# Two transformer blocks on one core: hi/lo pairs in SBUF start at multiples of 256 bytes instead of 128, and rows of the convolution's tile have 516 words instead of 515

## The reference

```python
def second_block(x, c, ...):
    for layer in range(2):
        x = sandwich(x, c_act, mixer, ...)   # layer 0: even_mixer, layer 1: odd_mixer
        x = sandwich(x, c_act, mlp, ...)     # square(relu(h @ w1)) @ w2, hidden width 4096
def even_mixer(h, w_in, ...):
    z, xbc, dt_raw, q, k, v = split_cols(h @ w_in, EVEN_SPLITS)
    y_ssd = ssd_mixer(z, xbc, dt_raw, ...)   # xbc = silu(causal_depthwise_conv(xbc, conv_w, conv_b)), 4 taps
    y_diff = diff_attention(q, k, v, ...)
    return concatenate([y_ssd, y_diff]) @ w_out
def odd_mixer(h, w_in, ...):
    rq, rk, rv, rg, sq, sk, sv = split_cols(h @ w_in, ODD_SPLITS)
    return concatenate([retention(rq, rk, rv) * silu(rg), sliding_window_attention(sq, sk, sv)]) @ w_out
```

## The kernel before

| pair | starts (hi, lo) | over a multiple of 512 | used by |
|---|---|---|---|
| `w_hi`, `w_lo` | 16896, 33280 | 0 | all |
| `hT`, first block | 91136, 107520 | 0 | first block |
| `oT` | 132096, 144384 | 0 | first block |
| `w_out_more` | 160640, 177024 | 384 | output projection, first block, twice |
| `xT`, `aT`, `w_more` | 170240, 190720, 194816 and on | 256 | experts |
| `hT`, second block (right) | 212864, 196480 | 384 | even projection, `conv_projection`, both `mlp`, odd projection |
| `normedT`, first (about 1974 to 2024 us) | 103552, 119936 | 128 | `norm_projection` after `diff_attention` |
| `normedT`, second (2256 to 2317 us) | 136448, 152832 | 256 | `norm_projection` after `ssd` |
| `normedT`, third (2949 to 3002 us) | 193664, 210048 | 128 | `norm_projection` after retention |
| `soT` | 136320, 144512 | 128 | `window_projection`, 96 matmuls |
| `hid` | 103424, 119808 | 0 | both `mlp` |

## Time and profile before

### The profile page before, as it was taken

How to read it: one execution, slowest core, us unless ns; L and a number is a source line. 1 busy time by engine, 2 the same in 40 slices (tenths; PEclk the granted TensorE clock), 3 DMA queues, 4 the chain that set the end, 5 groups by cost and what they waited for, 6 DMA issues and landing times. The chain is left out here.

```text
span 3482.8 us, 39412 instructions
## 1 busy us (share of the span) xinstructions
PE 3102.3 (89%) x14919; PEld 2518.6 (72%) x14919; DVE 2226.9 (64%) x3130; ACT 1231.3 (35%) x1668; POOL 391.4 (11%) x152
## 2 busy tenths in 40 slices
PE   4998989995799889999399799789999898889999
PEld 3877769774677778877386578668887687758887
DVE  6756674997676667698534646666665565554445
ACT  2234233774325224467223624431112322331112
POOL 0000001000000000000000000314443000014443
PEclk9999999997899999999599999889999899979999
DMA  7754633996645742799452042124442452113222
GB/s 255 248 193 147 221 116 120 408 403 252 233 146 186 243 164 87 305 398 364 175 184 69 25 139 91 55 91 142 139 142 84 141 174 76 55 49 97 96 91 78
DMA packets 284711, 581.81 MB, mean 167 GB/s; under 512 B 21241, under 2 KB 129473, under 8 KB 277500
## 3 DMA queue, kind: packets, MB, share of 16 engines
q1 hardware_dynamic: 272168, 535.90, 44.1%
q10 hardware_dynamic: 7764, 26.85, 1.9%
q0 software_dynamic: 4608, 16.78, 1.3%
HBM read 527.50 MB, written 78.71 MB: 174 GB/s over the span
## 5 line engine op out<-in xcount | busy, mean ns | idle before, releaser
L138 ACT CAST w_hi<-ring 128x2048 fp32r<-128x2048 f32 (+3 forms) x156 | 289.1, 1856 | 1174.2 <-PE ps L290 1037.3
L290 PE MATMUL ps<-hT_hi,w_hi 128*128 128x512 f32 (+1 forms) x1256 | 501.4, 399 | 27.3 <-DVEq L1124 16.0
L290 PE MATMUL ps<-hT_lo,w_hi 128*128 128x512 f32 (+1 forms) x1256 | 496.5, 395 | 0.0
L145 POOL TENSOR_TENSOR w_lo<-ring,w_hi 128x2048 fp32r<-128x2048 f32 x64 | 306.7, 4793 | 907.5 <-ACTq L3205 525.4
L150 DVE TENSOR_TENSOR w_lo<-ring,w_hi 128x2048 fp32r<-128x2048 f32 (+3 forms) x104 | 226.9, 2186 | 183.4 <-ACT w_hi L138 183.1
L290 PE MATMUL ps<-hT_hi,w_lo 128*128 128x512 f32 (+1 forms) x1256 | 306.3, 396 | 5.9 <-DVE w_lo L150 5.9
L290 PEld LDWEIGHTS ps<-hT_hi,w_hi 128*128 128x128 f32 (+1 forms) x1256 | 238.5, 190 | 87.4 <-DVEq L1124 17.6
L1061 DVE SCALAR_TENSOR_TENSOR piece_sums<-pieces,cond,piece_sums 128x512 f32<-128x512 f32 x294 | 220.7, 751 | 97.7 <-DMA pieces<-in_w_ada_dram 47.9
L290 PEld LDWEIGHTS ps<-hT_hi,w_lo 128*128 128x128 f32 (+1 forms) x1256 | 237.1, 189 | 62.5 <-DVE w_lo L150 7.2
L290 PEld LDWEIGHTS ps<-hT_lo,w_hi 128*128 128x128 f32 (+1 forms) x1256 | 238.5, 190 | 53.5
L290 PE MATMUL ps<-w_hi,hT_hi 128*128 128x512 f32 (+1 forms) x544 | 209.7, 388 | 0.0
(11 more groups left out here) (651 smaller groups left out, 6320.0 us busy)
## 6 DMA issues: line engine op xcount, KB each, us to landing
ring<-in_mlp_w_dram SPq DMA_DIRECT2D x64, 1024.0 KB, 5.0
pieces<-in_w_ada_dram SPq DMA_DIRECT2D x96, 512.0 KB, 6.3
ring<-in_w_in_dram SPq DMA_DIRECT2D x36, 1024.0 KB, 7.0
pieces<-in_mod_w_dram SPq DMA_DIRECT2D x72, 512.0 KB, 5.2
raw_sep<-in_w_exp_down_dram SPq DMA_DIRECT2D x24, 1024.0 KB
ring<-in_e_w_in_dram SPq DMA_DIRECT2D x24, 1024.0 KB, 5.3
slots_x<-const_zeros_dram SPq DMA_DIRECT2D x2, 11776.0 KB
raw_sep<-in_w_exp_gate_dram SPq DMA_DIRECT2D x46, 512.0 KB, 9.0
```

The lines of the kernel that those rows point to most:

```text
L138: self.k.nc.scalar.copy(self.k.parts[0][:, i, 0:words], self.k.ring[:, i, 0:words]).then_inc(self.high, 1)
L145: self.k.nc.gpsimd.tensor_tensor(self.k.parts[1][:, i, 0:words], self.k.ring[:, i, 0:words], self.k.parts[0][:, i, 0:words].bitcast(F32), ...
L290: mm = pe.matmul(out, a if weight_left else b, b if weight_left else a, start=first and part == 0 and q == ks[0] and o == 0, stop=last and ...
```

## The change

`pair_of` asks for starts at multiples of `2 * LINE` = 256 bytes. `xbc` gets rows of `LEAD + S` = 516 words, its zeros are words 1 to 3 and its tokens begin at word 4; every reader and writer moves along by one word, and the taps are read from words 1, 2, 3 and 4.

```diff
+LEAD = 4
 def pair_of(nc, c, name, shape, side=None):
-    return tuple(c.enter_context(on_chip(nc, fresh(name + e), shape, F32R, side=side)) for e in ("_hi", "_lo"))
+    return tuple(c.enter_context(on_chip(nc, fresh(name + e), shape, F32R, side=side, line=2 * LINE)) for e in ("_hi", "_lo"))
...
-                        mm = pe.transpose(k.ps[:, bank + q - q0, t * P:(t + 1) * P], xbc[:, q, 3 + t * P:3 + (t + 1) * P], k.ident[:])
+                        mm = pe.transpose(k.ps[:, bank + q - q0, t * P:(t + 1) * P], xbc[:, q, LEAD + t * P:LEAD + (t + 1) * P], k.ident[:])
...
-                nc.scalar.activation(cv[:, q % 3, :], xbc[:, q, 0:S], ACT.Identity, scale=taps[:, q:q + 1], bias=taps[:, 64 + q:65 + q]).then_inc(first_tap, 1)
+                nc.scalar.activation(cv[:, q % 3, :], xbc[:, q, LEAD - 3:LEAD - 3 + S], ACT.Identity, scale=taps[:, q:q + 1], bias=taps[:, 64 + q:65 + q]).then_inc(first_tap, 1)
...
-                nc.scalar.activation(xbc[:, q, 3:3 + S], cv[:, q % 3, :], ACT.Silu).then_inc(silu_done, 1)
+                nc.scalar.activation(xbc[:, q, LEAD:LEAD + S], cv[:, q % 3, :], ACT.Silu).then_inc(silu_done, 1)
...
-            V.memset(xbc[:, :, 0:3], 0.0).then_inc(taps_out, 1)
+            V.memset(xbc[:, :, LEAD - 3:LEAD], 0.0).then_inc(taps_out, 1)
...
-                    link(V.scalar_tensor_tensor(o, xbc[:, q, j:j + S], taps[:, 16 * j + q:16 * j + q + 1], o, ALU.mult, ALU.add))
-                V.scalar_tensor_tensor(o, xbc[:, q, 3:3 + S], taps[:, 48 + q:49 + q], o, ALU.mult, ALU.add).then_inc(conv_done, 1)
+                    link(V.scalar_tensor_tensor(o, xbc[:, q, LEAD - 3 + j:LEAD - 3 + j + S], taps[:, 16 * j + q:16 * j + q + 1], o, ALU.mult, ALU.add))
+                V.scalar_tensor_tensor(o, xbc[:, q, LEAD:LEAD + S], taps[:, 48 + q:49 + q], o, ALU.mult, ALU.add).then_inc(conv_done, 1)
...
-        BT = lambda ch, g: xbc[:, 8 + g, 3 + ch * P:3 + (ch + 1) * P]
-        CT = lambda ch, g: xbc[:, 12 + g, 3 + ch * P:3 + (ch + 1) * P]
+        BT = lambda ch, g: xbc[:, 8 + g, LEAD + ch * P:LEAD + (ch + 1) * P]
+        CT = lambda ch, g: xbc[:, 12 + g, LEAD + ch * P:LEAD + (ch + 1) * P]
...
-            xbc = d.enter_context(on_chip(nc, fresh("xbcT"), [P, 16, S + 3], F32))
+            xbc = d.enter_context(on_chip(nc, fresh("xbcT"), [P, 16, LEAD + S], F32))
```

More of the change, by code:

```diff
@@ L3030, in move_out @@
                     for m in (0, 1):
-                        last = nc.scalar.copy(xbc[:, tile(u, m), 3:3 + S], k.ps[:, 4 * (u % 2) + m, :])
+                        last = nc.scalar.copy(xbc[:, tile(u, m), LEAD:LEAD + S], k.ps[:, 4 * (u % 2) + m, :])
                 else:
@@ L3122, in move_out @@
                 for m in (2, 3):
-                    last = V.tensor_copy(xbc[:, tile(u, m), 3:3 + S], k.ps[:, 4 * (u % 2) + m, :])
+                    last = V.tensor_copy(xbc[:, tile(u, m), LEAD:LEAD + S], k.ps[:, 4 * (u % 2) + m, :])
                 last.then_inc(free_dve, 1)
```

## The result

The changed kernel takes 3460.67 us (median of six runs, 3451.43 to 3469.45). The kernel before, run beside it again, has a median of 3480.16 us over its six runs (3470.83 to 3484.52). The ratio is 0.9948 with a 95% interval of 0.9928 to 0.9968: faster, by 11 to 25 us. The forecast was 3460.0 us. The profiled execution of the changed kernel is the slowest of its six: 3469.45 us, with a span of 3467.7 us and a mean granted clock of 0.941, as in the profiled execution before.

The account below looks back on a forecast made before the run. PE's matmul pace was taken as the bound. Terms of 15.0 and 10.5 us made 25.5, less 0.5 and 0.4 us left 24.6, so 3484.6 became 3460 us; range 3453 to 3477.

Parts of the forecast that it names:

- The bound: Whole kernel: PE, busy 89% of the span, sets the streams' length; a nanosecond off each matmul is one off the span.
- The size of the term: 512-column matmuls on moved pairs: 2304 gain 6.5 ns, 1752 gain 6.0 ns; 25.5 us, or 24.6 after deductions.
- The 0.4 us: Third `normedT` stage: the gain on 60 matmuls before PE's waits for DVE's tiles is waited away, 0.4 us.
- Zero for part two: Convolution's tile with rows of 516 words: no gain taken, bounds 0.7 us either way on 48 taps.
- 129 lines become 128: Convolution's taps: by the 16-byte line rule rows of 516 words cross fewer lines, under 1% of a tap.
- 6 us either way: Stage starts, some 25: allowance for shifts in where stretches at 1.2 GHz end, four matmuls costing 0.8 us.
- The cause: Matmul streams: where the pair lies sets the pace; multiples of 256 are fast, 128 over them slow.
- theory 1: All matmul streams: a pair is fast when its own start is a multiple of 256, whatever the other operand's start.
- The reading on `w_more`: Experts: `w_more`, a moving operand at 256 over a multiple of 512, makes eight steps of 227 ns.
- A: Streams with `hT` moving: only the stationary side heals, features stay at 233.2 ns; 9.1 us saved, 3475.5 us; chance 0.11.
- B: All moved pairs: no effect, the pace follows something else that goes with the stage; 3484.6 us; chance 0.06.
- C: `hT` at 256 against `w_hi` at 0: a worse rhythm, 15 ns over 389 on 2424 matmuls; 3496 us; chance 0.03.

Follow-up runs that it names:

- pairs alone: The kernel before with only the pairs put at multiples of 256, rows of the convolution's tile kept at 515 words; 3462.75 us, ratio 0.9951.
- both again: The changed kernel, pairs at multiples of 256 and rows of 516 words, run once more against the kernel before; 3462.14 us, ratio 0.9956.
- everything at 128: The kernel before with `w_hi`, `w_lo`, `w_out_more`, `normedT` and `soT` moved so that all pairs lie 128 over a multiple of 256; 3463.62 us, ratio 0.9948.
- the parts moved: The kernel before with the weights' parts `w_hi` and `w_lo` moved to 128 over multiples of 256; 3453.93 us, ratio 0.9945.
- rows alone: The kernel before with only rows of 516 words, pairs left at multiples of 128; 3475.28 us, ratio 0.9988.
- the reverse kernel: The changed kernel with `w_hi` and `w_lo` moved to 128 over multiples of 256; 3489.15 us, ratio 1.0028 to the kernel before.
- the warmed kernel: The changed kernel with 18 matmuls of 128 columns on the identity before each `mlp`; 3472.28 us, ratio 0.9992 to the kernel before.

## Why the prediction was right, and where its reasons were not

**The bound: right.** PE sets the end of each stream; the streams shortened by what their matmuls did, but for the first `mlp` with its stretch at 1.2 GHz, and no new wait appeared in them. In the odd projection ACT's wait for the weights' DMA is 23.8 us (20.2 before); PE's matmuls still wait for nothing there and its weight loads 0.2 us.

**The size of the term: right.** 6.5 and 6.0 ns on 4056 matmuls, 24.6 us. Summed from start to start over the steps of the slow streams, what lies over 226.7 ns a matmul is 24.6 us in the trace before and 0.6 us in the trace after (steps at 2.4 GHz and under 300 ns, 3950 of the 4056). By streams, spread over all matmuls of each, it was 6.3 to 6.6 ns a matmul in the even projection and the two `mlp`, 6.0 for `w_out_more`, 5.7 and 5.8 in the convolution's and the odd projection, 4.8 to 5.4 for `soT` and `normedT`, so the 6.0 taken for these last was a little high. The 0.4 us that the third `normedT` stage was to wait away is there: its three waits for DVE went from 10.5 us to 10.7. The 256-column matmuls did not gain; their step went from 118.6 to 119.9 ns, 0.1 us lost over 96. Zero for part two held. The working that "129 lines become 128" is wrong for most taps, though: three of the four never start on a boundary in the new rows, so that over all taps as many cross as before.

**The sum against the measurement: right by a piece of luck.** The gain in medians was 19.5 us in the first comparison, and 14.3, 14.9 and 15.9 in those of pairs alone, both again and everything at 128; by their ratios these four are 15 to 18 us. 24.6 lies inside the interval of the first (11 to 25 us), at or just beyond the upper ends of the others (22 to 24 us). With the parts moved, where `w_out_more`, two `normedT` and `soT` stay slow and some 21 us were to be had, it was 23.1 in medians and 19 by the ratio. The time of 3460 was hit because the runs of before that it was worked out from lie high (3482 to 3484.6 us, against a median of 3479.5 over 29).

What is missing goes with the clock, a step that the prediction had only as 6 us either way. Over the 29 runs of the kernel before, 0.001 of mean granted clock goes with 2.8 us. The 31 runs of the four kernels with all these streams at 226.7 (changed, both again, pairs alone, everything at 128) had a mean clock of 0.9418; the 41 of the kernel before and of rows alone 0.9433. At an equal clock of 0.942 the lines through the two groups give 3461.1 and 3481.6, 20.5 us apart, and 4 us of them are given back. The 4 us between 20.5 and 24.6 aren't accounted for; the scatter about the two lines leaves only some 2 us either way for the 20.5.

In the profiled pair a part of the loss can be placed. From barrier to barrier the stage of the second `normedT` took 95.5 us in place of 90.1, with no edit near it, the first `mlp` lost some 5 us to the lower clock, and the experts of the second layer took 317.5 us in place of 312.9, with 10.2 us of PE's work at 1.2 GHz in place of none; two other stages won 3.3 and 4.9 us in the same way (the one after the convolution, 58.9 in place of 62.2, and the one before the last `mlp`, 60.7 in place of 65.6).

Whether the faster pace *causes* the lower clock stays open. For it speaks the reverse kernel, the slowest by its paces, with a mean clock of 0.9446 over ten runs, higher than that of the kernel before and of the changed one. The stage of the second `normedT` comes in two versions, 90.0 to 91.5 us with 17 to 18 us of PE's work at 1.2 GHz, or 95.5 with 31. The second is in the changed kernel, pairs alone, both again and everything at 128, but also in the kernel with `hid_hi` or `hid_lo` off, where all streams up to there have the pace of the kernel before; and the warmed kernel, which is the changed one up to that stage, has 90.0.

**The cause: wrong in its form.** "What sets the two apart is where the pair lies" took one operand's start for the rule, because the other operand was at a multiple of 512 in every row. It is the distance of the two. The rule fitted the kernel at hand and failed on the next one: the kernel with the parts moved would have been forecast slower by theory 1, and it is as fast as the changed one. What in the chip makes the distance count, no run here shows.

**The reading on `w_more`: right, and not typical.** The eight steps of 227 ns on `w_more` were steady because they came late in a stream without a break. Most streams of the experts are only 12 matmuls long and start after a wait or another instruction, and those have other medians, before and after the change, although `xT`, `aT`, `hT`, `w_more` and the parts all start at multiples of 256 there. From the trace after: the tile (duration min/median/max), then a late group (595.17 to 596.98 us, 8 steps of 226 ns) and one in a fresh stream (599.71 to 601.33, 7 steps of 231 ns):

```profile
L2443 PE MATMUL ps<-w_more_hi,xT_hi x176: 387/397/481, 595.2 to 1647.7; 128*128 128x512 f32 x176
...
595.17 0.39 PE L2443 MATMUL ps<-w_more_hi,xT_hi 128*128 128x512 f32 x1
...
596.98 1.07 PE L2446 MATMUL ps<-w_more_lo,xT_hi 128*128 128x512 f32 x4
...
599.71 0.39 PE L2443 MATMUL ps<-w_more_hi,xT_lo 128*128 128x512 f32 x1
...
601.33 1.09 PE L2446 MATMUL ps<-w_more_lo,xT_hi 128*128 128x512 f32 x4
```

Over the 130 streams of the experts the first ten steps after the restart average 230.1 ns; in the few that go on, the steps from the twelfth on are at 226.7. So agreeing starts give the fast pace only once a stream has run for some ten matmuls, and a median of 397 in short streams is no sign of a distance.

**The rivals.** *A*, that only the stationary side heals, falls: windows of features are at 227 ns. *B*, no effect, falls by pairs alone and by the paces. *C*, a worse rhythm of `hT` at 256 over 512 beside `w_hi` at 0, falls: 256 counts as no distance. A longer duration of single matmuls, from which *C* was priced, did not come: the longest with `hT_lo` on `w_out_more` is 395.

## What to carry to other kernels

Give the moving and the stationary operand of a stream of matmuls starts that agree modulo 256 bytes; it is the agreement that pays, not a rounder start of one of them. The sign is two paces for the same form at the same clock inside long streams (226.7 and 232 to 234 ns here, medians of 389 and 392 to 398), and moving one small thing low in the stack can heal or spoil all streams above it. Where a forecast rests on PE's pace alone, keep some of it back for the granted clock: here 14 to 20 us of 24.6 were seen in the medians with all these streams fast.

## What the runs showed of the hardware

- At 2.4 GHz a 512-column fp32r matmul in a long stream takes 226.7 ns from start to start when its operands' starts agree modulo 256 bytes. At a distance of 128 it takes 232.3 to 233.3, whichever side is off.
- At a distance of 64 it depends on the side: 233.3 with the moving operand 64 below the stationary one, 228.9 to 229.2 (230.4 in the first block's features) with it 64 above. At 32 below it is 233.3 (32 above not run).
- A matmul whose own operands agree pays too when it alternates with one whose operands don't (396 beside 396).
- In the experts, whose starts agree, the first ten steps after a restart average 230.1 ns.
- The start of a row on a one-word or 16-byte boundary changed no tap, transpose or copy by more than 4 ns in the median.
- In five profiled kernels PE worked 31 us at 1.2 GHz in the stage of the second `normedT`, in seven others 17 to 18 and in one 23; the two versions do not follow the edits.
